# Weight chunks of a two-layer fp32 trunk kept in rings of four places, with the low part written over the raw chunk

## What is computed

```python
def swiglu(x, w1, w3, w2):
    return (jax.nn.silu(x @ w1) * (x @ w3)) @ w2
...
    for i in range(DEPTH):
        h = h + 0.5 * swiglu(rmsnorm(h, ffn1_norm[i]), ffn1_w1[i], ffn1_w3[i], ffn1_w2[i])
        hn = rmsnorm(h, mix_norm[i])
...
        h = h + m
        h = h + 0.5 * swiglu(rmsnorm(h, ffn2_norm[i]), ffn2_w1[i], ffn2_w3[i], ffn2_w2[i])
        gate = jax.nn.sigmoid(rmsnorm(h, ple_norm[i]) @ ple_gate[i])
        h = h + (p[i].astype(h.dtype) @ ple_proj[i]) * gate
    return rmsnorm(h, final_norm)
```

## Time and profile before

| | us |
|---|---|
| median of three runs | 1079.1 |
| lowest, highest | 1078.89, 1080.94 |
| the profiled execution, whole | 1082.04 |
| its span, first to last instruction of the program | 1079.2 |
| TensorE busy in the span | 1062.9 |
| VectorE, ScalarE, GpSimd busy | 774.9, 606.5, 233.6 |

### The profile page before, as it was taken

How to read it: one execution, slowest core, us unless ns; L and a number is a source line. 1 busy time by engine, 2 the same in 40 slices (tenths; PEclk the granted TensorE clock), 3 DMA queues, 4 the chain that set the end, 5 groups by cost and what they waited for, 6 DMA issues and landing times.

```text
span 1079.2 us, 18816 instructions
## 1 busy us (share of the span) xinstructions
PE 1062.9 (98%) x7627; PEld 969.9 (90%) x7627; DVE 774.9 (72%) x913; ACT 606.5 (56%) x820; POOL 233.6 (22%) x227
## 2 busy tenths in 40 slices
PE   8999999999999999999999999999999999999997
PEld 7999999989998888888988888888998888888897
DVE  6778868879966777756787767566566777776576
ACT  6676645642365555544665555454777555554553
POOL 6899989220011000001120000011011200000020
PEclk9999999999999999999999999999999999999999
DMA  9555654432255665655555656656433456566552
GB/s 237 176 176 175 191 174 143 157 118 80 87 184 167 184 194 172 196 194 190 168 183 181 194 178 193 190 190 189 157 117 128 153 163 191 177 195 195 187 184 80
DMA packets 179678, 183.11 MB, mean 170 GB/s; under 512 B 16128, under 2 KB 173456, under 8 KB 179600
## 3 DMA queue, kind: packets, MB, share of 16 engines
q1 hardware_dynamic: 179456, 181.99, 54.4%
q10 hardware_dynamic: 144, 0.04, 0.0%
HBM read 180.95 MB, written 1.05 MB: 169 GB/s over the span
## 4 chain that ended last, share of the span: by engine, by line
PE 72%; DVE 3%; issue 2%; ACT 1%; POOL 0%; POOLq 0%; DVEq 0%; ACTq 0%
PE acc L1971 33%; PE acc L1973 17%; PE bank L1611 3%; PE bank L1612 3%; PE bank L1613 3%; PE acc L1611 2%; PE acc L1612 2%; PE acc L1613 2%; DVE w_lo L1058 1%; PE acc L1757 1%; DVE op_both L1071 1%; PE misc L1757 0%; PE acc L1862 0%; ACT w_hi L671 0%; PE stat L1791 0%
## 5 line engine op out<-in xcount | busy, mean ns | idle before, releaser
L1058 DVE TENSOR_TENSOR w_lo<-raw,w_hi 128x1024 fp32r<-128x1024 f32 x346 | 451.9, 1318 | 191.4 <-ACT w_hi L671 189.9
L671 ACT ACTIVATE w_hi<-raw 128x1024 fp32r<-128x1024 f32 x346 | 355.9, 1039 | 200.9 <-PE acc L1973 87.9
L1971 PE MATMUL acc<-op_both,w_hi 128*128 128x512 f32 x1056 | 374.7, 400 | 1.8 <-DVE op_both L1071 1.6
L1973 PE MATMUL acc<-op_both,w_lo 128*128 128x256 f32 x1056 | 296.1, 280 | 0.0
L1971 PEld LDWEIGHTS acc<-op_both,w_hi 128*128 128x128 f32 x1056 | 198.4, 188 | 52.4 <-DVE op_both L1071 2.4
L1973 PEld LDWEIGHTS acc<-op_both,w_lo 128*128 128x128 f32 x1056 | 199.4, 189 | 0.1
L1971 PE MATMUL acc<-g_all,w_hi 128*128 128x512 f32 x528 | 183.2, 392 | 0.0
L1611 PE MATMUL bank<-op_both,w_hi 128*128 128x256 f32 x584 | 170.5, 292 | 4.7 <-DVE op_both L1071 1.9
L1612 PE MATMUL bank<-op_both,w_lo 128*128 128x256 f32 x584 | 165.0, 283 | 0.0
L1613 PE MATMUL bank<-op_both,w_hi 128*128 128x256 f32 x584 | 165.0, 283 | 0.0
L1973 PE MATMUL acc<-g_all,w_lo 128*128 128x256 f32 x528 | 147.6, 280 | 0.0
(11 more groups left out here) (330 smaller groups left out, 1582.0 us busy)
## 6 DMA issues: line engine op xcount, KB each, us to landing
raw<-in_ffn_w_dram SPq DMA_DIRECT2D x258, 512.0 KB, 4.3
raw<-in_sb_w_qkv_dram SPq DMA_DIRECT2D x24, 512.0 KB, 3.5
raw<-in_s_w_glu_dram SPq DMA_DIRECT2D x16, 512.0 KB, 3.5
raw<-in_ple_gate_dram SPq DMA_DIRECT2D x16, 512.0 KB, 3.9
raw<-in_s_w_in_dram SPq DMA_DIRECT2D x8, 512.0 KB, 3.7
raw<-in_sb_w_o_dram SPq DMA_DIRECT2D x8, 512.0 KB, 3.4
raw<-in_ffn_w_dram SPq DMA_DIRECT2D x12, 256.0 KB, 3.1
raw<-in_ple_proj_dram SPq DMA_DIRECT2D x4, 512.0 KB, 3.5
```

What stands on the lines that cost most here:

```text
L671: act.activation(w_hi[:, slot, 0:width], raw[:, slot, 0:width], ACT.Copy).then_inc(hi_done, 1)
L1058: dve.tensor_tensor(w_lo[:, slot, 0:width], raw[:, slot, 0:width], w_hi[:, slot, 0:width].bitcast(F32), ALU.subtract).then_inc(lo_done, 1)
L1971: pe.matmul(pairs[h][:, m].rearrange("p i t -> p (i t)"), wh, x.rearrange("p i t -> p (i t)"), start=first, stop=False, skip_group_check=True)
L1973: return pe.matmul(pairs[h][:, m, 0, :], wl, x[:, 0, :], start=False, stop=last, skip_group_check=True)
```

## The change

Five things change.

- The rings have four places (`RING = 4`).
- `w_lo` lies at the address of `raw`: the subtraction writes the low part over the chunk that it reads. Two rings of four places take 32 KB of a partition where three rings of three took 36 KB.
- So a place of `raw` is free only when TensorE is through with the chunk in it: a load of chunk n waits for `pe_done`, and chunk n-4, in place of `lo_done` and chunk n-3.
- The loops `Fori` of the first SwiGLU block are written out as Python loops on all four engines, since six chunks to a group no longer come back to the same place of a ring of four.
- The copy of the product's high part into the first half of `g_hi` gets a wait of its own for `pe_done`, which the high part of a chunk ahead of it carried before.

```diff
-    RING = 3
+    RING = 4
...
-        w_lo = sb("w_lo", [P, RING, 1024], F32R)
+        w_lo = sb("w_lo", [P, RING, 1024], F32R, at=spot["raw"])
...
-                if not isinstance(n, int) or n >= RING:
-                    sp.wait_ge(lo_done, n - (RING - 1))
+                if n >= RING:
+                    sp.wait_ge(pe_done, n - (RING - 1))
...
-                with sp.Fori(2, NG) as g:
+                for g in range(2, NG):
...
                 def do_g_hi(g, half):
                     act.wait_ge(prod_done, base + g + 1)
+                    if g and half == 0:
+                        act.wait_ge(pe_done, n0 + 6 * g + 4)
...
-                    split_hi(n + j, m % RING, g * 2 + (m // RING + 1))
+                    split(n + j)
...
-                with dve.Fori(1, NG - peeled(nxt)) as g:
+                for g in range(1, NG - peeled(nxt)):
...
-                with pe.Fori(2, NG - peeled(nxt)) as g:
+                for g in range(2, NG - peeled(nxt)):
```

More of the change, by code:

```diff
@@ L368, in pair @@
                     for half in range(2):
-                        load(n + half, (s + half) % RING, a_chunk(w, half, bass.ds(g * 256, 256)), True)
+                        load(n + half, (n + half) % RING, a_chunk(w, half, slice(g * 256, g * 256 + 256)), True)
                 def down(n, s, g):
                     for j in range(2):
-                        load(n + j, (s + j) % RING, w2[bass.ds(g * 256 + j * P, P), :], False)
+                        load(n + j, (n + j) % RING, w2[g * 256 + j * P:g * 256 + j * P + P, :], False)
                 pair(w1, st.n0, st.n0, 0)
@@ L718, in part @@
                 def part(n, j, g):
-                    m = n0 + j - 2
                     if nxt.kind == "s5" and isinstance(n, int):
                         take_turned(n + j - 3 - n0)
-                    split_hi(n + j, m % RING, g * 2 + (m // RING + 1))
+                    split(n + j)
                     if nxt.kind == "s5" and isinstance(n, int):
@@ L750, in ffn @@
                 else:
-                    with act.Fori(1, NG - peeled(nxt)) as g:
+                    for g in range(1, NG - peeled(nxt)):
                         group(g)
@@ L1193, in part @@
                 def part(n, j):
-                    split_lo(n + j, (n0 + j - 2) % RING)
+                    split(n + j)
                     if nxt.kind == "s5" and isinstance(n, int):
@@ L2048, in up, with down_tile @@
                     for half in range(2):
-                        chunk_a(n + half, (s + half) % RING, half, bank[which], u, **kw)
+                        chunk_a(n + half, (n + half) % RING, half, bank[which], u, **kw)
                         behind(n + half)
-                def down_tile(s, m, j, half):
-                    wh, wl = (w[:, (s + j) % RING, m * P:(m + 1) * P] for w in (w_hi, w_lo))
+                def down_tile(n, m, j, half):
+                    wh, wl = (w[:, (n + j) % RING, m * P:(m + 1) * P] for w in (w_hi, w_lo))
                     return products(acc[m // 2][:, m % 2, :], wh, wl, g_hi[:, half, j, :], g_lo[:, half, j, :], False, False)
@@ L2063, in down @@
                         for m in range(KD):
-                            mm = down_tile(s, m, j, half)
+                            mm = down_tile(n, m, j, half)
                         mm.then_inc(pe_done, 1)
```

## The result

| | before | changed |
|---|---|---|
| first comparison, median of 8 and 8 runs | 1080.53 us | 1086.3 us (1081.79 to 1087.79), ratio 1.0057, 95% interval 1.0042 to 1.0072 |
| second comparison, 35 and 10 runs | 1081.7 us | 1085.73 us (1083.17 to 1089.91), ratio 1.0036, interval 1.0022 to 1.0051 |
| span of the profiled execution | 1079.2 us | 1085.8 us |

The forecast was 1083.1 us in a range of 1079.8 to 1090.5 us. The direction and the range held; the sum was 3.2 us short. Of that, 1.4 us are the starting point (1079.1 us from three runs, 1080.5 us from eight), and 1.8 us are the change itself: 5.8 us where 4.0 were forecast.

The account below looks back on a forecast made before the run. TensorE bounds the kernel, busy 1062.9 of 1079.2 us. Up parts, loops and start 0, entries into stages 2.7, long loads 1.3 sum to +4.0 us: forecast 1083.1 us, range 1079.8 to 1090.5 us.

Parts of the forecast that it names:

- The gate's new place: High parts that wait for TensorE: the load waits for chunk n-4, then takes 3.5 us; some 0.6 to 0.7 us later.
- Up parts 0: Up parts of the SwiGLU blocks: the later landing stays hidden, even with a transfer of 4.6 us; cost 0.
- chunk 118's kind: First chunk of each up-part group of four, high part behind the silu: its margin of 0.6 us stays.
- The subtraction over its own input, 0: VectorE's low part written over the chunk it reads: length unchanged at 1.23 us, cost 0.
- Entries, three times +0.6 us: Into the first gate stage, attention and the second gate stage: the whole VectorE chain moves, +0.6 us each.
- four places: Both gate-stage entries, into attention and out of attention: the later landing is not hidden, together 2.7 us.
- Out of attention, +0.9 us: Chunk 268's load lands 1.2 us later, some 0.3 us is won back ahead: +0.9 us.
- Long loads, +1.3 us: Nine down-part places, four entries, some chunks elsewhere: one load in five long, 2.0 us at most, +1.3 us taken.
- half chunks break a chain of long transfers: Argument against long transfers keeping themselves up (+12.5 us, chance 0.17): half chunks and every stall break the chain.
- the load of 6.56 us: Load issued at 355.45, its high part started at 362.01; cited to show single loads can be long without a neighbour.
- Loops, 0: First SwiGLU block: writing the loops out can save no more than 0.4 us of TensorE's idle time; taken as 0.
- Timed runs lie at the span: Timed runs (median 1079.1 us) lie at the profiled span of 1079.2 us, so the sum starts from there.

Follow-up runs that it names:

- experiment 6: Changed kernel with five places for the low part and four for the high: ratios 0.9977, 0.9951 to the kernel before; with six and three: 0.9958.
- experiment 4: Changed kernel with GpSimd's four additions of squares at the end of attention cut from 256 columns to 1: 1083.06 us beside 1081.62 for the kernel before.
- experiment 7: Changed kernel with 12 or 24 more empty TensorE matmuls at the start: 1087.04 us (ratio 1.0047) and 1087.31 us (1.0054) to the kernel before.
- experiment 3: Changed kernel with chunk 268 made behind the operand's parts of j = 1 on ScalarE and VectorE: 1084.56 us, ratio 1.0027 to the kernel before.

## Why the prediction was right, and where its sum was off

- **The gate's new place (+0.7 us for the high part): right.** SyncE's loads wait for TensorE, the median is 3.5 us, and the high parts wait for landings.
- **Up parts 0: right but for one chunk.** No new wait in the groups; chunk 118's kind stays covered. Only chunk 288, in a row of seven long loads, took 0.4 us more. What differs is the pace (below), which the changed kernel shares with the others.
- **The subtraction over its own input, 0: right**, by experiment 6.
- **Entries, three times +0.6 us.** Measured +0.3 and +0.3 (chunk 160), +0.9 and +1.0 (238), +0.6 and +0.5 (338): together 1.8 and 1.7 us for 1.8. Chunk 238 is more, where the load of chunk 237 took 3.7 and 3.8 us; chunk 160 is less, likely because the stalls of 154 to 156 lie ahead of it: it is 0.4 to 0.8 us where those are small or absent (experiments 4 and 7).
- **The way out of the gate stage was left out.** The prediction lists four places and says that all are entries; chunk 169 is a fifth of the same kind, VectorE's chain with landings in it. It cost 0.9 and 1.0 us in the changed kernel, and 0.8 us with a short load of chunk 167 (experiment 7).
- **Out of attention, +0.9 us: the mis-sized term.** Measured +3.3 and +3.7. The step that failed is the one that moved VectorE's chain with its lengths unchanged. The landing was late by the 1.2 us of the prediction (1.2 to 1.6 us in the traces), and experiment 3 shows that much without the rest; two pairs of `op_both` instead of one met GpSimd's additions, 1.0 us (experiment 4), and in both traces TensorE's clock fell behind these waits, some 1.2 to 1.7 us more (the traces with 12 and 24 more matmuls have the waits but not the fall, and take 12.8 and 13.0 us for the three chunks).
- **Long loads, +1.3 us: too small.** Measured +2.5 and +2.3 at 154 to 156 and 220, 221, and in the second trace 0.8 more at 325 to 327. The prediction said that half chunks break a chain of long transfers. That is the step that failed: half chunks start them. It also put the stall at one long transfer in five by chance, where in the traces it went with two loads close together and an instruction transfer in the first. And it took the load of 6.56 us for one without a neighbour: the trace of before has a load 2.5 us ahead of it, which landed 2.2 us after its issue, and another 2.4 us behind it.
- **Loops, 0: wrong.** They give some 2 us. In the kernel with the loops alone they also cost 0.9 at chunk 169: the load of chunk 167, with an instruction transfer beside it, took 4.8 us (3.5 before), and behind it VectorE's pair meets an addition of GpSimd.
- **The sum.** By comparison the rings cost 6.4 us and the loops give 2.4 back, 4.0 together in that comparison and 5.8 in the first; forecast was 4.0 and 0. That the total is near is in part luck: two errors have opposite signs.
- **"Timed runs lie at the span": wrong.** Each run lies 1.7 us or more above its own span (up to 3.0 before, up to 1.8 with the loops written out); the three runs at hand were on the low side. It cost the forecast 1.4 us, by the median of eight.

## What to carry to other kernels

Count a ring in the time between the release that starts a transfer and the use of its data, not in places: storing over the source moves the release from the next step to the last one. Where a chain has no slack, look up what runs on the engine that shares its memory port, since a shift of 1 us can bring an operation beside one that makes it longer. And before the smaller ring is taken, try unequal rings in the same space: here five places for the raw chunk and low part with four for the high part, or six with three, were both faster than three of each.

## What the runs showed of the hardware

- **TensorE has two paces at full clock.** The same eight pairs of matmuls take 2.77 or 2.83 us. In the changed kernel, two neighbouring chunks' first matmuls in two up parts:

```profile
398.77 0.40 PE L1972 MATMUL acc<-op_both,w_hi 128*128 128x512 f32 x1
...
401.54 0.40 PE L1972 MATMUL acc<-op_both,w_hi 128*128 128x512 f32 x1
```

```profile
598.84 0.40 PE L1972 MATMUL acc<-op_both,w_hi 128*128 128x512 f32 x1
...
601.67 0.40 PE L1972 MATMUL acc<-op_both,w_hi 128*128 128x512 f32 x1
```

  A pace lasts for tens of chunks and changes at a stall, for instance at chunk 180 of the kernel before. It differs between executions: the up part from chunk 90 on is mostly fast in the first trace of five and four (37 chunks of 43) and mostly slow in the second (2 of 43), with the same instructions. A whole up part at the other pace is 2.5 us, more than most of the losses above; this may explain much of the spread of 7 us among runs of one kernel, and it is why I compared steps and not stages. What sets it stays open.
- **The clock fell in two of four traces** with the same waits near 862 us, and TensorE was no busier in the two where it did not fall (busy for 4.23 and 4.29 of the 7 us before 862, against 4.26 and 4.47). In other traces it fell once near 197 or 224 us, in the first block's end or the S5 stage. So these waits cost 1.2 to 1.7 us more in some executions and not in others; what decides it stays open.
- **A load takes some 3.5 us alone and some 4.6 us (4.0 to 5.0) when it follows another within 1.6 us.** At a spacing of 2.8 us both can keep themselves up: chunks 285 to 291 of the changed kernel took 4.4 to 4.7 us each, one behind the other.
